# A two-block transformer on one core: where dense matmuls stand between the sums of the first stick-breaking layer

## The reference, cut to what matters

```python
def stick_breaking_attention(q, k, v):
    for i in range(S // BLOCK):                       # blocks of 128 queries, kl keys
        z = einsum('bthd,bshd->bhts', q[:, t0:kl], k[:, :kl]) * scale
        mask = s_idx < t_idx
        log_fail = where(mask, log_sigmoid(-z), 0.0)
        later = cumsum(log_fail, axis=3, reverse=True) - log_fail
        a = where(mask, exp(log_sigmoid(z) + later), 0.0)
        outs.append(einsum('bhts,bshd->bthd', a, v[:, :kl]))

def stick_breaking_layer(x, norm_g, w_in, w_out):
    q, k, v, gate = split(rms_norm(x, norm_g) @ w_in, 4)   # w_in is 1024 x 4096
    o = stick_breaking_attention(q, k, v)
    return x + (o * silu(gate)) @ w_out
```

## Time and profile before

| what | value |
|---|---|
| three runs, median (lowest to highest) | 1832.68 us (1830.98 to 1833.95) |
| the profiled execution, device time | 1835.86 us |
| its span in the profile | 1834.0 us |
| PE busy | 98% of the span, 10340 matmuls |
| DVE, ACT, POOL busy | 63%, 47%, 25% |
| mean granted clock of TensorE | 0.995 of full speed |
| the pairs of the first layer | from about 115 us to 300 us of the span |

### The profile page before, as it was taken

One profiled execution on the slowest core, in us unless ns is written; L12 is line 12 of the kernel. 1 busy time (PEld: TensorE's weight loads), 2 busy tenths in 40 slices (PEclk: granted clock), 3 DMA queues, 4 the chain that ended last, 5 costly groups with the idle time before them and its releaser, 6 DMA issues.

```text
span 1834.0 us, 26208 instructions
## 1 busy us (share of the span) xinstructions
PE 1789.8 (98%) x10340; PEld 1460.4 (80%) x10340; DVE 1150.3 (63%) x1861; ACT 866.9 (47%) x1409; POOL 450.9 (25%) x451
## 2 busy tenths in 40 slices
PE   7999999999999999999999999999999999999997
PEld 6877777775678757677879898988888787989896
DVE  5355556575546688854578575765677657858574
ACT  5236665455435465564345252633445434435253
POOL 0035551101311235560140000005678214000000
PEclk9999999999999999999999999999999999999999
DMA  5321111231013411111232322222222123232322
GB/s 177 101 78 49 47 47 58 80 101 50 24 47 100 133 60 34 36 36 58 80 122 86 115 93 104 93 97 83 84 88 76 46 81 127 81 115 92 106 91 80
DMA packets 44521, 149.20 MB, mean 81 GB/s; under 512 B 6000, under 2 KB 6384, under 8 KB 44400
## 3 DMA queue, kind: packets, MB, share of 16 engines
q1 hardware_dynamic: 44400, 147.53, 24.1%
HBM read 139.64 MB, written 2.10 MB: 77 GB/s over the span
## 4 chain that ended last, share of the span: by engine, by line
PE 85%; DVE 6%; ACT 4%; POOL 2%; issue 2%; DMA 1%; POOLq 0%; SPq 0%; DVEq 0%; ACTq 0%
PE BANK L301 18%; PE BANK L303 17%; PE BANK L302 17%; PE BANK L2405 4%; PE BANK L2404 4%; PE BANK L2402 4%; PE BANK L955 3%; PE BANK L688 2%; PE BANK L1739 1%; PE BANK L1720 1%; DMA WRAW<-in_wc 1%; DVE WL L278 1%; PE BANK L1696 1%; PE BANK L1012 1%; PE BANK L2710 1%
## 5 line engine op out<-in xcount | busy, mean ns | idle before, releaser
L269 ACT ACTIVATE WH<-WRAW 128x1024 fp32r<-128x1024 f32 (+1 forms) x214 | 223.0, 1044 | 340.8 <-PE BANK L303 306.0
L278 DVE TENSOR_TENSOR WL<-WRAW,WH 128x1024 fp32r<-128x1024 f32 (+1 forms) x201 | 256.3, 1276 | 138.8 <-ACT WH L269 138.6
L301 PE MATMUL BANK<-HH,WH 128*128 128x512 f32 x664 | 273.1, 411 | 12.1 <-DVE WL L278 9.8
L303 PE MATMUL BANK<-HL,WH 128*128 128x512 f32 x664 | 260.2, 392 | 0.0
L302 PE MATMUL BANK<-HH,WL 128*128 128x512 f32 x664 | 259.9, 391 | 0.0
L301 PE MATMUL BANK<-HIDH,WH 128*128 128x512 f32 (+1 forms) x520 | 201.2, 387 | 1.6 <-issue 1.5
L302 PE MATMUL BANK<-HIDH,WL 128*128 128x512 f32 (+1 forms) x520 | 200.7, 386 | 0.0
L303 PE MATMUL BANK<-HIDL,WH 128*128 128x512 f32 (+1 forms) x520 | 200.7, 386 | 0.0
L2405 PE MATMUL BANK<-HP,G 128*128 128x256 f32 x672 | 190.2, 283 | 0.0
L2404 PE MATMUL BANK<-HP,G 128*128 128x256 f32 x672 | 190.2, 283 | 0.0
L2402 PE MATMUL BANK<-HP,G 128*128 128x256 f32 x672 | 190.1, 283 | 0.0
(11 more groups left out here) (446 smaller groups left out, 3694.2 us busy)
## 6 DMA issues: line engine op xcount, KB each, us to landing
WRAW<-in_w SPq DMA_DIRECT2D x77, 512.0 KB, 3.5
WRAW<-in_wd SPq DMA_DIRECT2D x64, 512.0 KB, 3.5
RAW<-in_wf SPq DMA_DIRECT2D x32, 512.0 KB, 3.6
WRAW<-in_wu SPq DMA_DIRECT2D x16, 512.0 KB, 3.5
TMP<-in_wf SPq DMA_DIRECT2D x16, 512.0 KB, 3.5
WRAW<-in_w0o SPq DMA_DIRECT2D x8, 512.0 KB, 3.5
WRAW<-in_w1o SPq DMA_DIRECT2D x8, 512.0 KB, 3.4
WRAW<-in_wc SPq DMA_DIRECT2D x8, 512.0 KB, 3.5
```

Of the source, the lines that this page charges most:

```text
L269: e.activation(WH[b % NS][:, 0:n], WRAW[b % NR][:, 0:n], ACT.Copy).then_inc(*inc("s_high", ("high", b)))
L278: e.tensor_tensor(WL[b % NS][:, 0:n], WRAW[b % NR][:, 0:n], WH[b % NS][:, 0:n].bitcast(F32), ALU.subtract).then_inc(*inc("s_low_pool" if p ...
L301: e.matmul(dst, ah, bh, start=first and i == 0, stop=False)
L303: made = e.matmul(dst, ah, bl, start=False, stop=last and i == len(sets) - 1)
```

## The change

In pairs 1 to 5 nine eighths instead of eight stand ahead of the first sums, three instead of four between the two sums, and four behind them as before. In pair 0 there are fourteen instead of twelve ahead, three instead of four between, three instead of four behind. In pair 6, which has no dense tile left but l0k 7, slice 0 of the output projection's tile 0 goes ahead of the first sums, two slices stand between the sums, and one behind them. No instruction is added or taken away.

```diff
--- before.py
+++ after.py
@@ -712,18 +712,19 @@
                 logits(m)
                 if m:
                     values(m - 1)
-                eighths(8 if m else 12)
+                eighths(9 if m else 14)
                 sums(2 * m)
-                eighths(4)
+                eighths(3)
                 sums(2 * m + 1)
-                eighths(4)
+                eighths(4 if m else 3)
             logits(6)
             values(5)
             eighths(8)
+            planes(0, 0)
             sums(12)
-            planes(0, 0, 1)
+            planes(0, 1, 2)
             sums(13)
-            planes(0, 2, 3)
+            planes(0, 3)
             logits(7)
             values(6)
             planes(0, 4, 5)
```

## The result

The changed kernel takes 1838.32 us, the median of nine runs (1837.11 to 1839.5), against 1833.48 us for nine runs of the kernel before (1830.98 to 1836.3): 4.8 us more, ratio 1.0027 with a 95% interval of 1.0019 to 1.0036. Slower, as forecast, and inside the range.

A forecast was written before the change was run, and what follows sets the result against it. PE, busy for 98% of the span, was taken as the bound. Pairs 1 to 5 (+4.40), pair 6 (+1.36) and pair 0 (−1.02) summed to +4.74 us, giving 1837.4 us by the median; range 1834.8 to 1840.6.

The forecast's parts named there:

- pair 0: First pair: no wait for bank 7, two more eighths fill the idle time ahead of the sums, logits 1.02 us sooner.
- pairs 1 to 5, each: Second sums, and so the logits, come 0.88 us later per pair; five pairs make +4.40 us.
- pair 6: Output projection's slice 0 waits for bank 7 behind l0k 7; the logits of pair 7 come 1.36 us later.
- The ninth eighth waits for the eviction of l0k m+1: Pairs 1 to 5: both tiles use bank 7, so it starts after DVE's eviction ends at 173.69, not at 172.35.
- Rival 1: The wait for bank 7 costs nothing and the edit fills idle time: −4.1 us, 1828.6 us; chance 0.06.
- the prediction's pair without a wait: Pairs 1 to 5 if bank 7 costs no wait: second sums at 177.85, 0.61 us earlier than 178.46.
- Its price: Wait for the eviction in pairs 1 to 5: 0.88 us each, bounded by 0.38 below and 1.47 above.
- Weight loads: At PE's waits, a load starts with its matmul; were it pulled ahead, six waits would cost some 0.6 us less.
- Weigh has slack: ACT in pairs 1 to 5: first weigh not held up, 1.33 us of slack before the logits, second's distance unchanged.
- Rival 3, a slow cast ahead of the eviction: DVE cast takes 1.02 instead of 0.43 us, 1.47 per pair: +8.3 us, 1841.0 us; chance 0.06.
- Rival 2, something given back: PE catches up within a pair or in later layers: +2.2 us, 1834.9 us; chance 0.18.
- The clock: TensorE's clock doesn't fall: 1.45 us idle in pair 0 left it at 1.00, new waits of 1.23 are no longer.

The follow-up runs named there:

- e5: The changed kernel with DVE's eviction of l0k m+1 ahead of the first cut of head 2m+1, pairs 1 to 6: 22.79 us per pair, ratio to before 1.0013.
- e6: The changed kernel with DVE's eviction of l0k m+1 behind the second cut of head 2m+1, pairs 1 to 6: 1852.74 us, ratio to before 1.0108.
- e7: The kernel before with 10 eighths ahead, 2 between, 4 behind in pairs 1 to 5: 23.27 to 23.29 us per pair, ratio 1.0026.
- e8: The kernel before with tiles shifted one eighth against the pairs, `values(m - 1)` at the border, weight splits moved: 1829.59 us, ratio to before 0.9984.
- e1: The kernel before with only pair 0 changed (14, 3, 3 eighths): 1831.47 us, ratio 0.9994; logits 0 to 1 take 22.68 us.
- e9: e8's program with one eighth fewer ahead of the first sums and one more between them: 24.67 us per pair, ratio 1.006.

## Why the prediction was right

| term | forecast | measured |
|---|---|---|
| pair 0 | −1.02 | −0.98 |
| pairs 1 to 5, each | +0.88 | +0.99 |
| pair 6 | +1.36 | +1.56 |
| sum over the pairs | +4.74 | +5.51 |
| whole kernel | +4.74 (1837.4 us) | +4.84 (1838.32 us, medians) |

- *The ninth eighth waits for the eviction of l0k m+1*: shown by the rows, by e5 and e6, which change only the eviction's place on DVE and move the pair's time with it, and by e7, where the tenth eighth is free. Rival 1, that the wait costs nothing, would have given 1828.6 us; e8 comes near it by another order (1829.59), and the prediction's pair without a wait (0.61 us saved) is 0.51 there.
- *Its price*: 0.11 low per pair. The handover from the eviction to the matmul was taken as 0.05 from the earlier trace rows and measures 0.15 in each of pairs 1 to 5 (173.11 to 173.26). In pair 6 it is 0.21, and that is most of the 0.20 by which pair 6 was too low. From the eighth to the second sums it was 0.77 + 2.73 + 2.13 = 5.63 where 0.80 + 2.69 + 2.11 = 5.60 was forecast.
- *Weight loads*: no load was pulled ahead into the wait. The one of the ninth eighth starts at 173.23 and its matmul at 173.26, so the row was the right one to go by. No matmul was in flight at the end of this wait, so the rows say nothing of a load behind a running one. The restart costs less than taken, though: 0.77 to the next start and not 0.80.
- *Weigh has slack*: ACT's first weigh stayed where it was, 16.6 us behind the logits, and the second follows the sums 2.90 behind their start. Logits follow the second sums by 5.60, before 5.59.
- *Pair 0*: the sums of head 1 start at 132.89, when POOL's last cut ends at 131.19 + 1.65 = 132.84. e1 has it alone.
- *Rival 3, a slow cast ahead of the eviction*, didn't happen in the changed kernel but did in e6, with 0.99 for 0.43 us.
- *Rival 2, something given back*: by the medians 0.7 of 5.5 us, which is less than they can tell: the interval of the ratio reaches from 3.5 to 6.6 us. The profiled executions show nothing given back up to 1421 us, where the lag is still 5.2 us.
- *The whole*: that the medians differ by 4.84, 0.1 from the forecast, is partly luck. The terms add up to 0.8 us too little, and the median of before is 0.8 higher over nine runs than over the three that the forecast started from (1833.48 and 1832.68; in the experiments, with 31 and 24 runs, it was 1832.23 and 1832.45).
- *The clock*: as forecast, it stayed at 1.00 in the pairs. The reason given, that a wait of 1.45 us had left it alone, was too weak: in the same trace it fell at 1421 us, where the waits just ahead were of 1.07 and 0.23 us.

Open: why the handover takes 0.15 us here, 0.21 in pair 6 and 0.05 in the earlier trace rows. No run was made for it.

## What to carry to other kernels

Filling a wait on the bounding engine with work moved ahead is worth only what that work itself need not wait for: look at which buffer its first instruction takes, who frees it, and where in that engine's queue this stands. A wait that stood under other work costs nothing until the work above it is moved away; here a border between two tiles in one bank needed the sums above it. Where the border can be moved under other work instead (e8, with `values` in between), the same fill brings its gain, in this case 2.9 us by the medians.

## What the runs showed that was not expected

- Behind waits of 2.97 us (3.03 in pair 6) TensorE's clock fell to half in three pairs of six and stayed in the others (e6), for 1.56 us each; waits of 1.34 to 1.40 us never did in the pairs. Late in the trace of before, and in that of e8, it fell behind waits of 1.07 and 0.23 us, which stand in the changed kernel too and did nothing there. In the traces of before and of the changed kernel it also fell for some 4 us at 762 and at 768 us, at a wait of 1.51 us, and in that of e1 it did not, with the same wait. So the length of the last wait doesn't decide it alone.
- An instruction can also stand too early in an engine's queue. In e9 DVE waited 3.51 us at the eviction for the end of the tile, with the cuts that POOL and the second sums need behind it, and a pair took 2.39 us more than before; in the changed kernel, where the eviction comes late and nothing on DVE is held, it took 0.99 more.
- A single profiled execution can hide more than half of a change of 5 us: a stretch of some 7 us at half clock, far behind the changed code, lay in one of the two and not in the other, and took 3.0 us.
